# Windowed attention of a two-block transformer kernel, regrouped into four units of eight heads and one token tile

## What is computed

```
def swa_layer(h, k_sh, v_sh, wq, q_gain, sinks, wo):
    q = (h @ wq).reshape(B, T, N_Q_HEADS, HEAD_DIM)      # 16 heads of 64
    q = rms_norm_2(q, q_gain) * (HEAD_DIM ** -0.5)
    return swa_sink_attention(q, k_sh, v_sh, sinks) @ wo

def shared_kv(x, kv_norm, w_kv, k_gain):                 # 2 key/value heads
    kv = (rms_norm_2(x, kv_norm) @ w_kv).reshape(B, T, 2, N_KV_HEADS, HEAD_DIM)
    k = rms_norm_2(kv[:, :, 0], k_gain)
    v = kv[:, :, 1]

# swa_sink_attention, WINDOW = 128:
    s = jnp.where(valid, q k^T - slope * dist, -inf)
    m = max(max(s), sink)
    p = exp(s - m) / (sum(exp(s - m)) + exp(sink - m))
    o = p v
```

## Time and profile before

| | |
|---|---|
| median of 3 runs | 1628.0 us (1622.14 to 1630.01) |
| the profiled execution | 1627.13 us, span 1625.2 us |
| PE busy | 1430.6 us, 88% of the span |
| PEld busy | 1164.8 us, 72% |
| DVE busy | 886.7 us, 55% |
| ACT busy | 703.8 us, 43% |
| POOL busy | 68.4 us, 4% |
| mean granted TensorE clock | 0.934 |

### The profile page before, as it was taken

How to read it: one execution, slowest core, us unless ns; L and a number is a source line. 1 busy time by engine, 2 the same in 40 slices (tenths; PEclk the granted TensorE clock), 3 DMA queues, 4 the chain that set the end, 5 groups by cost and what they waited for, 6 DMA issues and landing times.

```text
span 1625.2 us, 22432 instructions
## 1 busy us (share of the span) xinstructions
PE 1430.6 (88%) x8294; PEld 1164.8 (72%) x8294; DVE 886.7 (55%) x1245; ACT 703.8 (43%) x1120; POOL 68.4 (4%) x51
## 2 busy tenths in 40 slices
PE   5999999888978899997679499889999984799998
PEld 3888878666767778886556488847888873578887
DVE  3545467865543454546456854444655567455554
ACT  4344465453444444435333322223544553644443
POOL 0000000000000000000004101200000001000000
PEclk9999999888999999998889799969999997799999
DMA  6646546234434555554214000022655632135553
GB/s 216 217 163 201 187 154 216 97 124 143 130 108 151 133 175 175 189 199 163 83 65 140 3 3 28 18 91 65 197 187 185 216 122 79 30 126 183 192 181 117
DMA packets 145715, 221.43 MB, mean 136 GB/s; under 512 B 16828, under 2 KB 65096, under 8 KB 145512
## 3 DMA queue, kind: packets, MB, share of 16 engines
q1 hardware_dynamic: 145640, 220.40, 41.5%
HBM read 219.30 MB, written 1.05 MB: 136 GB/s over the span
## 4 chain that ended last, share of the span: by engine, by line
PE 80%; DVE 11%; ACT 5%; issue 2%; POOL 1%; DMA 1%; SPq 0%; ACTq 0%; DVEq 0%
PE gp L268 11%; PE acc L268 11%; PE acc L269 11%; PE acc L270 11%; PE gp L269 11%; PE gp L270 11%; PE tp L831 1%; DVE sb_w_lo L262 1%; PE tp L1767 1%; PE acc L2005 1%; PE gp L1989 1%; PE tp L449 1%; PE acc L2002 1%; ACT sb_arena L2477 1%; ACT sb_xa_hi L427 1%
## 5 line engine op out<-in xcount | busy, mean ns | idle before, releaser
L262 DVE TENSOR_TENSOR sb_w_lo<-sb_raw,sb_w_hi 128x1024 fp32r<-128x1024 f32 x400 | 479.2, 1227 | 267.0 <-ACT sb_w_hi L251 266.2
L251 ACT ACTIVATE sb_w_hi<-sb_raw 128x1024 fp32r<-128x1024 f32 x400 | 410.3, 1059 | 308.4 <-PE acc L270 160.3
L268 PE MATMUL gp<-sb_w_hi,sb_xa_hi 128*128 128x512 f32 (+1 forms) x736 | 296.7, 403 | 28.4 <-DVE sb_xa_lo L434 13.5
L269 PE MATMUL gp<-sb_w_hi,sb_xa_lo 128*128 128x512 f32 (+1 forms) x736 | 290.7, 395 | 0.0
L270 PE MATMUL gp<-sb_w_lo,sb_xa_hi 128*128 128x512 f32 (+1 forms) x736 | 290.4, 395 | 0.0
L268 PEld LDWEIGHTS gp<-sb_w_hi,sb_xa_hi 128*128 128x128 f32 x736 | 142.2, 193 | 62.5 <-issue 16.7
L270 PEld LDWEIGHTS gp<-sb_w_lo,sb_xa_hi 128*128 128x128 f32 x736 | 141.9, 193 | 30.3
L269 PEld LDWEIGHTS gp<-sb_w_hi,sb_xa_lo 128*128 128x128 f32 x736 | 142.4, 194 | 27.7
L268 PE MATMUL acc<-sb_w_hi,sb_mid_hi 128*128 128x512 f32 x408 | 159.1, 390 | 0.0
L270 PE MATMUL acc<-sb_w_lo,sb_mid_hi 128*128 128x512 f32 x408 | 158.9, 389 | 0.0
L269 PE MATMUL acc<-sb_w_hi,sb_mid_lo 128*128 128x512 f32 x408 | 158.7, 389 | 0.0
(11 more groups left out here) (361 smaller groups left out, 1849.1 us busy)
## 6 DMA issues: line engine op xcount, KB each, us to landing
sb_raw<-in_ffn_w SPq DMA_DIRECT2D x264, 256.0 KB, 4.3
sb_raw<-in_mlp_w SPq DMA_DIRECT2D x256, 256.0 KB, 2.9
sb_raw<-in_w_in SPq DMA_DIRECT2D x72, 256.0 KB, 3.4
sb_raw<-in_a_w_rkv SPq DMA_DIRECT2D x48, 256.0 KB, 3.8
sb_raw<-in_xattn_w_kv SPq DMA_DIRECT2D x32, 256.0 KB, 3.5
sb_raw<-in_w_out SPq DMA_DIRECT2D x16, 256.0 KB, 3.0
sb_raw<-in_xattn_w_q SPq DMA_DIRECT2D x16, 256.0 KB, 5.6
sb_raw<-in_xattn_w_o SPq DMA_DIRECT2D x16, 256.0 KB, 4.0
```

What stands on the lines that cost most here:

```text
L251: A.e.activation(w_hi[:, s], raw[:, r], ACT.Copy).then_inc(hi_done, 1)
L262: V.e.tensor_tensor(w_lo[:, s], raw[:, r], w_hi[:, s].bitcast(F32), ALU.subtract).then_inc(lo_done, 1)
L268: e.matmul(dst, xh, wh, start=start, stop=False)
L269: e.matmul(dst, xl, wh, start=False, stop=False)
```

## The change

The sixteen heads and two tiles become four units, each with half the heads (b) of one tile (t). Below they are called U0 to U3, in the order of `UNITS`. `GROUPS` says which heads of a unit share a PSUM bank.

- The query rows are no longer copied. ACT squares them from PSUM per unit (`act_square`), DVE sums eight heads (`dve_ss`), POOL takes the power of eight columns, and one DVE instruction reads PSUM and multiplies by the row scale and the head scale (`dve_q`).
- Query gain, key gain and 1/8 are folded into one column of 128 numbers (`gain_q`), which ACT applies as the scale of the copy from PSUM to the query columns (`act_q_cols`). SP loads it with four small DMAs in place of two.
- The queries of `q[0]` are turned to columns before `q[1]` is multiplied, the keys in the middle of it. `q[1]` is made by tile. Logits of U0 and U1 are between or behind its chunks.
- Logits, bias, maximum, Exp, division, turning and the product with the values are written unit by unit, with the units shifted against each other.
- Block 0 of `out` is made by tile: tile 0 after the second unit of tile 0 (U2), tile 1 after U3.
- In `PreNorm` with two targets, the eight columns of XA are now all made before those of XB.

```diff
             def act_token(self, A, t, *targets):
-                for k in range(self.kts):
-                    A.e.wait_ge(self.turned, self.turned0 + 2 * t + k // 4 + 1)
-                    for x, gain in targets:
+                for n, (x, gain) in enumerate(targets):
+                    for k in range(self.kts):
+                        if n == 0:
+                            A.e.wait_ge(self.turned, self.turned0 + 2 * t + k // 4 + 1)
+                        else:
+                            A.e.wait_ge(*self.done_at(self.kts * (self.sets * t + n - 1) + 4 * (k // 4 + 1)))
...
+            UNITS = ((0, 0), (1, 0), (0, 1), (1, 1))
+
+            GROUPS = (((0, 2, 4, 6), (1, 3, 5, 7)), ((0, 2), (1, 3), (4, 6), (5, 7)))
...
             def pe(self, T):
-                self.q[0].pe_first(T, 0, XA, lambda t: acc[:, t, 0:512], self.pre.turn, mlp1_add.h_at)
+                self.pre.turn.pe_token(T, 0, h_rows, mlp1_add.h_at(0))
+                self.pe_q(T, 0, 0, range(0, 3))
+                self.pre.turn.pe_token(T, 1, h_rows, mlp1_add.h_at(1))
+                self.pe_q(T, 0, 0, range(3, 4)).then_inc(*T.one(self.q_half))
+                self.pe_q(T, 0, 1, range(0, 4))
                 self.kv.pe(T, 0, XB, lambda t: gp[:, t, :], self.pre.turn.complete())
...
+                self.pe_q_turn(T, 0)
+                self.pe_q(T, 1, 0, range(0, 4)).then_inc(*T.one(self.q_half))
+                T.e.wait_ge(self.k_ready, NT + 1)
...
+                mm.then_inc(*T.one(self.turned))
+                self.pe_q(T, 1, 1, range(0, 2))
+                self.pe_logits(T, 0)
+                self.pe_q(T, 1, 1, range(2, 4))
+                self.pe_logits(T, 1)
+                self.pe_q_turn(T, 1)
+                self.pe_p(T, 0)
+                self.pe_logits(T, 2)
+                self.pe_o(T, 0)
+                self.pe_p(T, 1)
+                self.pe_o(T, 1)
+                self.pe_logits(T, 3)
+                self.pe_p(T, 2)
+                self.pe_o(T, 2)
+                T.e.wait_ge(*stage(self.o_done, 3))
+                self.pe_out(T, 0)
+                self.pe_p(T, 3)
+                self.pe_o(T, 3)
+                T.e.wait_ge(*stage(self.o_done, 4))
+                self.pe_out(T, 1)
                 self.out.pe_by_token(T, 1, XB, lambda t: acc[:, t, 512:1024], (self.o_done, 4))
...
+                self.act_q_cols(A, 0)
+                split_hi(A, self.q[1].end)
+                self.act_square(A, 1, 0)
+                A.e.wait_ge(self.turned, 3)
+                A.e.activation(self.k_cols.rearrange("p g s -> p (g s)"), gp[:, 0, :], ACT.Copy).then_inc(*A.one(self.cols))
+                split_hi(A, self.out.first[0] + 2)
+                self.act_exp(A, 0)
+                self.act_square(A, 1, 1)
+                self.act_exp(A, 1)
+                self.act_q_cols(A, 1)
+                self.act_p(A, 0)
+                split_hi(A, self.out.first[0] + 4)
...
+            def dve_q(self, V, b, t):
+                n = 2 * b + t
+                V.e.wait_ge(self.rstd, self.norm_of_q(b, t))
...
+                V.e.scalar_tensor_tensor(hd(self.row_of_q(t, b)), hd(self.q_bank(t, b)), self.pre.rstd(t),
+                                         self.ss_q[:, 8 * n:8 * n + 8].unsqueeze(2).to_broadcast([P, 8, HD]), ALU.mult, ALU.mult).then_inc(*V.one(self.q_rows))
...
+            def dve(self, V):
+                split_lo(V, self.kv.first[0] + 2)
...
+                self.dve_ss(V, 0, 0)
+                split_lo(V, self.kv.end)
+                self.dve_q(V, 0, 0)
+                self.dve_ss(V, 0, 1)
+                split_lo(V, self.q[1].first[0] + 2)
+                self.dve_q(V, 0, 1)
+                self.dve_k_squares(V)
+                split_lo(V, self.q[1].end)
+                self.dve_k(V)
+                self.dve_ss(V, 1, 0)
+                split_lo(V, self.out.first[0] + 2)
+                self.dve_q(V, 1, 0)
+                self.dve_bias(V, 0)
+                self.dve_ss(V, 1, 1)
+                self.dve_norm(V, 0)
+                self.dve_q(V, 1, 1)
+                self.dve_bias(V, 1)
+                split_lo(V, self.out.first[0] + 4)
+                self.dve_norm(V, 1)
+                self.dve_bias(V, 2)
+                self.dve_o(V, 0)
+                self.dve_o(V, 1)
+                split_lo(V, self.out.first[0] + 6)
+                self.dve_norm(V, 2)
+                self.dve_bias(V, 3)
+                self.dve_o(V, 2)
+                self.dve_norm(V, 3)
+                self.dve_o(V, 3)
```

More of the change, by code:

```diff
@@ L2455, in act_take_q, with norm_of_q, q_bank @@
-            def act_take_q(self, A, b):
-                split_hi(A, self.q[b].end + 4)
-                A.e.wait_ge(chunk_used, self.q[b].end)
-                for t in range(NT):
-                    A.e.activation(rows(2)[:, t, b * 512:(b + 1) * 512], acc[:, t, b * 512:(b + 1) * 512], ACT.Copy,
-                                   scale=self.pre.rstd(t)).then_inc(*A.one(self.q_taken[b]))
+            NORM_OF_K = 3
+            def norm_of_q(self, b, t):
+                return 3 * b + t + 1
+            def q_bank(self, t, b):
+                return acc[:, t, b * 512:(b + 1) * 512]
@@ new lines, in act_square, with act_q_cols @@
+            def act_square(self, A, b, t):
+                n = 2 * b + t
+                A.e.wait_ge(*((self.q_half, b + 1) if t == 0 else (chunk_used, self.q[b].end)))
+                if b:
+                    A.e.wait_ge(self.ss, self.norm_of_q(0, t))
+                A.e.activation(self.squares[t], self.q_bank(t, b), ACT.Square, scale=self.pre.rstd(t)).then_inc(*A.one(self.squared))
+            def act_q_cols(self, A, b):
+                A.e.wait_ge(self.k_ready, 1)
+                for n in range(2):
+                    A.e.wait_ge(self.turned, 3 * b + n + 1)
+                    A.e.activation(self.q_cols[:, 4 * b + 2 * n:4 * b + 2 * n + 2, :].rearrange("p k s -> p (k s)"), tp[:, n, :], ACT.Copy,
+                                   scale=self.gain_q[:, 0:1]).then_inc(*A.one(self.cols))
@@ new lines, in act_exp @@
+            def act_exp(self, A, n):
+                t, b = self.UNITS[n]
+                A.e.wait_ge(*stage(self.maxed, n + 1))
+                for head in range(8):
+                    at = 8 * n + head
+                    lg = self.logits[t][b][:, head, :]
+                    A.e.activation(lg, lg, ACT.Exp, bias=self.neg_max[:, at:at + 1], accum_out=self.sums[:, at:at + 1]).then_inc(*A.one(self.exped))
+                s = self.e_sink[:, 8 * n:8 * n + 8]
+                A.e.wait_ge(self.sink_in, n + 1)
+                A.e.activation(s, s, ACT.Exp).then_inc(*A.one(self.exped))
@@ new lines, in act_p, with o_at @@
+            def act_p(self, A, n):
+                t, b = self.UNITS[n]
+                at, count = self.P_TURNS[n]
+                for x in range(count):
+                    c, g = divmod(x, 2)
+                    A.e.wait_ge(*stage(self.p_turned, at + x + 1))
+                    A.e.activation(self.p_col[t, c][:, 8 * b + 4 * g:8 * b + 4 * g + 4, :].rearrange("p h q -> p (h q)"), tp[:, g, :], ACT.Copy).then_inc(*A.one(self.p_done))
+            def o_at(self, n):
+                t, b = self.UNITS[n]
+                return slice(None), slice(4 * b, 4 * b + 4), slice(t * P, (t + 1) * P)
@@ new lines, in act, with dve_ss @@
+                split_hi(A, self.out.end)
+                split_hi(A, ahead(self.out, 4))
+            def dve_ss(self, V, b, t):
+                n = 2 * b + t
+                s = self.ss_q[:, 8 * n:8 * n + 8]
+                V.e.wait_ge(self.squared, n + 1)
+                V.e.tensor_reduce(s, self.squares[t].rearrange("p (h d) -> p h d", d=HD), AX, ALU.add).then_inc(*V.one())
+                V.e.wait_ge(*V.last)
+                V.e.tensor_scalar(s, s, 1.0 / HD, EPS, ALU.mult, ALU.add).then_inc(*V.one(self.ss))
@@ new lines, in dve_norm @@
+            def dve_norm(self, V, n):
+                t, b = self.UNITS[n]
+                s = self.sums[:, 8 * n:8 * n + 8]
+                V.e.wait_ge(*stage(self.exped, 9 * (n + 1)))
+                V.e.tensor_tensor(s, s, self.e_sink[:, 8 * n:8 * n + 8], ALU.add).then_inc(*V.one())
+                V.e.wait_ge(*V.last)
+                V.e.reciprocal(s, s).then_inc(*V.one())
+                V.e.wait_ge(*V.last)
+                x = self.logits[t][b]
+                V.e.tensor_tensor(x, x, s.unsqueeze(2).to_broadcast([P, 8, self.KEYS[t]]), ALU.mult).then_inc(*V.one(self.normed))
```

325 lines of the change are left out of this document (165 added, 160 removed).

## The result

The changed kernel takes 1636.6 us (median of 6 runs, 1635.1 to 1638.3) against 1629.0 of the kernel before in the same runs (6 runs, 1622.1 to 1630.1): ratio 1.0056, 95% interval 1.0042 to 1.0071. Run again later, the changed kernel had 1.0065 (1.0045 to 1.0085). The profiled execution took 1637.5, with a span of 1635.7 us.

The account below looks back on a forecast made before the run. The attention stage was taken as bound by the length of one chain through DVE, ACT and PE. Chain +5.6 and clock +3.9 made +9.5 us: 1627.1 to 1636.6 profiled, 1637.5 as median, range 1625 to 1648.

Parts of the forecast that it names:

- Where the time goes: Window attention stage, 121.3 us before: its chain's length counts, the rest is untouched; stage length near 131 us if right.
- Part 1: Start of the stage, XA columns made before XB: counted 0, bounds 0 and 0.7 us gained.
- Part 2: Queries turned before `q[1]`: new PE wait of 2.9 us, U0's logits done at 1349.3, old 18 us block gone.
- Part 3: Chain of the four units through DVE, ACT and PE to the end of `out`: 1436.9 for 1431.3, +5.6 us.
- Part 4: PE's clock from U1's logits to U2's values and tile 0 of `out`: +3.9 us, bounds 0 and 6.
- The clock did not hold: Rival: scattered work keeps PE at 2.4 GHz; +5 us or less, about 1632, down to 1628; chance 0.22.
- Units did not overlap: Rival: in the attention DVE never waits for an Exp; 23 us less, 1605; chance 0.06.
- Hand-overs: Rival: about 40 in the chain, some 25 before; at 0.1 us more each, +4 and more clock, 1643; chance 0.15.

Follow-up runs that it names:

- e1: The kernel before with only the change to PreNorm's column order (all XA columns before XB): 1625.0 us, ratio 0.9995.
- e8: The changed kernel with 118 unread products filled into PE's waits, up to tile 0 of the output product: 1631.8 us, ratio 1.0036.
- e2: The changed kernel with the late token half's square before U0's Exps and its row scaling before U0's division: 1634.5 us, ratio 1.0050.
- e6: The changed kernel with the late half's square ahead, and U1's bias and maximum before U0's division: 1631.1 us, ratio 1.0030.
- e7: The changed kernel with the same instructions reordered on DVE, ACT and PE so that all four units overlap: 1605.4 us, ratio 0.9874.
- e5: The changed kernel run once more, unaltered, against the kernel before: 1637.6 us, ratio 1.0065.

## Why the prediction was right, step by step

Marks are counted on the old profile's clock, as in the prediction; the changed profile's have 2.6 added.

- **Where the time goes.** The stage was said to become near 131 us and became 133.9. Nothing outside it moved (from its end to the end of the span 193.9 us before, 194.3 after).
- **Part 1**, counted 0: right (e1), for another reason than I gave. I said that all of it ends in the wait for POOL's row scale, and took that scale to come no sooner. It comes 1.5 us sooner, the product behind it starts 1.1 us sooner, and the lower clock spends that.
- **Part 2**: PE's wait 2.10 for 2.9; U0's logits end at 1349.3, as said. The unknown operation from PSUM, 0.7 by bound, took 0.75. POOL's power of 8 columns, 1.8 by proportion, took 2.56 twice and then 1.64 twice. That the mark was met is partly luck: DVE's list began 1.1 us sooner than I took from the old rows (the gain of Part 1), and two waits of 0.40 for POOL, which I had not counted, used up most of it.
- **Part 3**: U1's bias at 1360.7 for 1360.3; query columns done 1371.4 for 1371.0; U1's division 1380.1 for 1378.6; U2's Exps 1386.6 for 1385.3. The end was put at 1436.9 with the clock left out. With the waits filled (e8) it is 1435.80 - 1308.48 + 1310.01 = 1437.3. So the chain was +6.0 for +5.6, or a little less, since e8's clock is not full everywhere. That it is this chain, and that order makes it, e2, e6 and e7 show: -2.7, -6.4, -29.8 for calls moved and nothing removed.
- **Part 4** is the term that was mis-sized: the clock, +3.9 by choice, between 0 and 6. Filling took 6.6 us off, more than the high bound. I had added up 4.9 and struck 1.0 as hidden under DVE, and that was wrong. Against e8, counted from the stage's start, the changed kernel loses 1.6 us ahead of U1's value products (I had 0.4 for transposes: a group of eight of U0's takes 1.94 for 1.06, of U1's 1.97 for 1.14), 1.7 in those products (said: 1.8), 0.9 in U2's (said: 0.9) and 2.3 in tile 0 of `out`, which takes 7.9 from 1410.5 to 1418.4 of its own profile (said: 1.8). The sum was +9.5 and the profiles' difference +12.6: 6.0 and 6.6. The two parts come from one run, e8, so that they add up proves nothing by itself; the marks above are the test of the first, the halved pieces of the second.
- **The base.** That 1637.5 met the median is luck, two errors that met: the difference was 3 us short by the profiles, and the old kernel's median, 1628.0 in the three runs shown, is 1625.8 in the 63 later ones. Against those the changed kernel is 12.0 us slower (e5), not 7.7.
- **Rivals.** The clock did not hold: 0.50 from 1360 to 1373 of the changed profile. Units did not overlap: U2's bias started there at 1377.5, with the end of U1's division. The price I gave that rival, 1605 us if DVE never waited, is the time of e7, 1605.4, but that too is partly luck: the price stands for a stage of 98 us on a base of 1628, and e7's stage is 104.2 on a base of 1625.6. Hand-overs cost little more than the old rows show, or the chain would not have come to 6.0 for 5.6.

## What to carry to other kernels

Cutting work into units overlaps nothing by itself: on engines that run in order, the list must put the next unit's first step ahead of this unit's last. Here one exchange was worth 3.7 us and all of them 30, some clock among it. And where PE works in short pieces between waits, count its pieces at the lower clock in full, the first product after them too; a cheap test is to fill the waits with products that nobody reads.
